# Scaling the attention probabilities on GpSimd instead of VectorE

## The reference

```python
# for each of 4 blocks of 128 queries, 16 heads of 64
logits = einsum("bqhd,bkhd->bhqk", q_blk, kf) * scale
logits = logits + (cq_blk[..., :, None] - ck[:, :, None, :])
logits = where(kpos <= qpos, logits, NEG_INF)
p = softmax(logits, axis=-1)
o = einsum("bhqk,bkhd->bqhd", p, vf)
```

## Time and profile before

| | |
|---|---|
| median of 3 runs | 2271.0 us (2269.18 to 2271.35) |
| the profiled execution, its time | 2272.01 us |
| its span | 2270.2 us |
| granted TensorE clock, mean | 0.996 |
| TensorE busy | 2247.9 us (99%) |
| VectorE busy | 1278.5 us (56%) |
| ScalarE busy | 819.6 us (36%) |
| GpSimd busy | 1.4 us (0%) |

### The profile page before, as it was taken

The page is one execution under the profiler, slowest core; times in us unless marked ns, Lnnn a source line. Parts: engine busy times, 40 slices in busy tenths (PEclk is TensorE's granted clock), DMA queues, the critical chain, the costliest instruction groups (busy, mean ns, idle before and its releaser), DMA issues.

```text
span 2270.2 us, 27725 instructions
## 1 busy us (share of the span) xinstructions
PE 2247.9 (99%) x10130; PEld 1845.0 (81%) x10130; DVE 1278.5 (56%) x1820; ACT 819.6 (36%) x1125; POOL 1.4 (0%) x6
## 2 busy tenths in 40 slices
PE   9999999999999999999999999999999999999998
PEld 7788878778888888888888888888888888888887
DVE  8878784758555345646454455555335555553544
ACT  6676473635333212224222223233212233221222
POOL 0000000000000000000000000000000000000000
PEclk9999999999999999999999999999999999999999
DMA  5233212122223222232322223222222232222322
GB/s 179 95 102 107 90 46 85 64 79 93 75 74 101 94 102 93 92 102 84 111 94 93 102 91 104 75 75 88 98 94 101 91 102 96 94 92 102 102 93 74
DMA packets 59507, 211.62 MB, mean 93 GB/s; under 512 B 6736, under 2 KB 7120, under 8 KB 59280
## 3 DMA queue, kind: packets, MB, share of 16 engines
q1 hardware_dynamic: 59040, 208.83, 27.2%
q0 software_dynamic: 224, 1.31, 0.2%
q10 hardware_dynamic: 144, 0.12, 0.0%
HBM read 208.14 MB, written 2.10 MB: 93 GB/s over the span
## 4 chain that ended last, share of the span: by engine, by line
PE 85%; DVE 2%; ACT 1%; issue 0%; DVEq 0%; ACTq 0%
PE bank L634 25%; PE bank L636 25%; PE bank L635 25%; PE bank L629 2%; PE bank L630 2%; PE bank L631 2%; PE bank L848 2%; ACT arena L1150 1%; PE bank L808 1%; PE bank L837 1%; PE bank L794 1%; PE bank L859 0%; DVE arena L1635 0%; DVE y_lo L1604 0%; PE bank L776 0%
## 5 line engine op out<-in xcount | busy, mean ns | idle before, releaser
L1298 DVE TENSOR_TENSOR w_lo<-w_raw,w_hi 128x1024 fp32r<-128x1024 f32 x387 | 467.6, 1223 | 775.3 <-ACT w_hi L934 774.4
L934 ACT ACTIVATE w_hi<-w_raw 128x1024 fp32r<-128x1024 f32 x387 | 403.9, 1057 | 944.8 <-PE bank L636 915.9
L634 PE MATMUL bank<-h_hi,w_hi 128*128 128x512 f32 x1788 | 701.2, 392 | 5.0 <-DVE arena L1333 2.0
L635 PE MATMUL bank<-h_lo,w_hi 128*128 128x512 f32 x1788 | 696.4, 389 | 0.0
L636 PE MATMUL bank<-h_hi,w_lo 128*128 128x512 f32 x1788 | 696.2, 389 | 0.0
L634 PE MATMUL bank<-y_hi,w_hi 128*128 128x512 f32 x1056 | 411.0, 389 | 1.6 <-DVE w_lo L1298 1.3
L636 PE MATMUL bank<-y_hi,w_lo 128*128 128x512 f32 x1056 | 410.8, 389 | 0.0
L635 PE MATMUL bank<-y_lo,w_hi 128*128 128x512 f32 x1056 | 410.8, 389 | 0.0
L634 PEld LDWEIGHTS bank<-h_hi,w_hi 128*128 128x128 f32 x1788 | 336.1, 188 | 77.8 <-DVE w_lo L1298 4.9
L635 PEld LDWEIGHTS bank<-h_lo,w_hi 128*128 128x128 f32 x1788 | 336.1, 188 | 70.9 <-issue 1.7
L636 PEld LDWEIGHTS bank<-h_hi,w_lo 128*128 128x128 f32 x1788 | 336.0, 188 | 70.3
(11 more groups left out here) (216 smaller groups left out, 1401.0 us busy)
## 6 DMA issues: line engine op xcount, KB each, us to landing
w_raw<-in_stream SPq DMA_DIRECT2D x389, 512.0 KB, 3.3
x<-in_x_t SPq DMA_DIRECT2D x8, 256.0 KB, 7.3
out_t<-x SPq DMA_DIRECT2D x8, 256.0 KB, 2.2
arena<-in_consts POOLq DMA_DIRECT2D x1, 1024.0 KB, 5.2
w_raw<-in_stream SPq DMA_DIRECT2D x2, 256.0 KB, 4.8
arena<-in_positions POOLq DMA_DIRECT2D x1, 256.0 KB, 6.2
vec_t<-in_vecs ACTq DMA_DIRECT2D x1, 112.5 KB, 3.1
ident<-in_consts SPq DMA_DIRECT2D x1, 64.0 KB, 6.9
```

Of the source, the lines that this page charges most:

```text
L634: pe.matmul(out, w_hi[:, slot, w], a_h, start=first, stop=False)
L635: pe.matmul(out, w_hi[:, slot, w], a_l, start=False, stop=False)
L934: A.activation(w_hi[:, slot, :], w_raw[:, slot, :], ACT.Copy).then_inc(hi_ready, 1)
L1298: V.tensor_tensor(w_lo[:, slot, :], w_raw[:, slot, :], w_hi[:, slot, :].bitcast(F32), ALU.subtract).then_inc(lo_ready, 1)
```

## The change

The four multiplications of each head move from VectorE's `normalise` into a new function `scale_probs` of GpSimd, which is called once at the start of each half of the attention. The reciprocal stays on VectorE and raises a new semaphore, `sums_inverted`, by one for each head; GpSimd waits for it and does the four multiplications, each of which raises `probs_ready` by one. `turn` now waits for four of these for each head instead of five.

```diff
+        sums_inverted = sem("sums_inverted")
...
         def _(pool):
             T = Tally()
+
+            def scale_probs():
+                for hh in range(HEADS // 2):
+                    sm = 32 * (hh % 2)
+                    pool.wait_ge(sums_inverted, T.value("halves", hh + 1, HEADS // 2))
+                    for t in range(TT):
+                        at = P * t * (t + 1) // 2
+                        p_t = probs[:, hh % 2, at:at + P * (t + 1)]
+                        nc.gpsimd.tensor_scalar(p_t, p_t, small[:, sm + 12 + t:sm + 13 + t], None, ALU.mult)\
+                            .then_inc(probs_ready, 1)
+
             for item in steps:
+                if isinstance(item, Bind) and item.name == "half" and not T.loops and T.fixed["halves"] < 2:
+                    scale_probs()
...
                 def turn(hh):
-                    pe.wait_ge(probs_ready, heads(5, 5 * hh + 5))
+                    pe.wait_ge(probs_ready, heads(4, 4 * hh + 4))
...
                 def normalise(hh):
                     sm = 32 * (hh % 2)
                     dve.wait_ge(exp_ready, heads(4, 4 * hh + 4))
-                    V.reciprocal(small[:, sm + 12:sm + 16], small[:, sm + 8:sm + 12]).then_inc(probs_ready, 1)
-                    dve.wait_ge(probs_ready, heads(5, 5 * hh + 1))
-                    for t in range(TT):
-                        at = P * t * (t + 1) // 2
-                        p_t = probs[:, hh % 2, at:at + P * (t + 1)]
-                        V.tensor_scalar(p_t, p_t, small[:, sm + 12 + t:sm + 13 + t], None, ALU.mult)\
-                            .then_inc(probs_ready, 1)
+                    V.reciprocal(small[:, sm + 12:sm + 16], small[:, sm + 8:sm + 12]).then_inc(sums_inverted, 1)
```

## The result

The changed kernel takes 2306.91 us (2306.41 to 2307.36, 4 runs) against 2270.31 (2269.18 to 2271.35, 4 runs) for the one before: a ratio of 1.0159, 95% interval 1.0147 to 1.0172, 36.6 us slower. The forecast was 2281 in 2270 to 2312; direction and range held, the size did not, a loss of 10 forecast and 37 measured.

What follows compares the result with a forecast made beforehand. The prediction took TensorE, 99% busy, to bound the kernel. Per half, 4 x 1.53 - 3 x 0.58 = 4.4, twice 8.8 us; with 1.65 for one clock fall, 2271.0 + 10.4 gave 2281, range 2270 to 2312.

Steps and rivals of the forecast that it cites:

- A to B: Leg from an even head's transposes' start to the next odd head's: 3.43 us before, predicted 4.96, 1.53 longer.
- D: Time of one head's four scalings on GpSimd, 1280 columns in all; estimated 2.7 us, against 1.27 on VectorE.
- the even leg: From an odd head's transposes' start to the next even head's: 6.19 us before, predicted 5.61, hiding the even head's scaling.
- rival 2: Scaling so slow (D over 3.35) that it sets both legs: 2308 at D = 5, 2358 at 8.6; chance 0.2.
- signs of being wrong: D outside 2.2 to 3.3, the clock falling at each pair, or the values product still ending the wait before odd heads.
- 1.6 ns a column, D = 2.05 + 0.62 = 2.7: GpSimd's scaling of a head, put between VectorE's two-input subtract (1.04 ns a column) and its scan (2.06).
- The clock: TensorE's granted clock falling toward 1.2 GHz after idling before odd heads; one fall over six such places booked, 1.65 us.
- rival 3: The clock falls before every odd head: six more falls at 1.65, 9.9 us on top of 8.8, 2290; chance 0.12.
- Head 0: First head of each half: scaling hidden behind the v product's tail and copies, cost 0; 1.0 us at risk from subtracts.
- The 0.58 us: Predicted shortening of each leg from odd to even head, 6.19 to 5.61, as VectorE's maxima start earlier.
- Rival 4: VectorE and GpSimd hold each other up, maxima run after the scaling as now: 3.5 us more, 2285; chance 0.05.

## Why the prediction was right in direction and wrong in size

**The chain held.** "A to B becomes D + 2.26": with the measured 4.27 that is 6.53, and the trace has 6.48. That D under 3.35 hides behind the even leg, and that above it both legs are D + 2.26, was rival 2, and it is what happened (6.41 to 6.47). The formula with D = 4.27 gives 8 x 3.1 + 6 x 0.34 = 26.8; the legs without the clock show 5.3 + 18.3 + 1.7 = 25.3. The kernel with its clock held is 26.7 slower than before by the medians and 24.6 by the spans, but that it comes so near is in part luck: it has head 0's loss in it, and it is spared the fall behind head 7, 1.5 and 1.2 us in the two halves, that the kernel before pays. That 2307 lies in the range is no merit of the sum either: the high end, 2312, stood for a D of 5 with two or three falls, and it was 4.27 with five. Of the prediction's own signs of being wrong two came true, D outside 2.2 to 3.3 and falls at nearly every pair.

**The step that failed is the price D**, the term "1.6 ns a column, D = 2.05 + 0.62 = 2.7". It measured 2.5 ns a column and 0.29 a piece, 4.27 in a row: above the scan's 2.06, well below the reciprocal's 6.2. I put an engine that had shown no row between two rows of a different engine, and took the middle of them as if it were likely; what the trace supported was only the wide bound. This term alone made 25.3 out of 8.8, 16.5 us of the miss; the clock, 6.5, and head 0, 1.6, are the rest of the 24.7 by the spans. The rule in the Trainium skill, "GPSIMD Engine Reference", section "Engine selection", that one-input work is at roughly line rate on GpSimd, is not borne out: by it, with the page's clock of 1.2 GHz, 1280 columns would take 1.07 us (an estimate), and 3.7 times that was measured even with a constant scalar. Its other half, that elementwise work belongs on VectorE, held: the ratio here was 4.27 to 1.27.

**The clock**, booked as one fall, 1.65, was 8.1 over the kernel before (6.7 in the legs, 1.4 behind head 7). The price of a fall was about right, 0.7 to 2.0 a leg; their number was not, five of six legs. The idle stretch was 3.1 us and not 1.6, and behind the stretches of 1.07 to 1.77 us that the kernel with odd heads' reciprocals ahead had, no fall came. So the number followed from D: rival 3 came true on top of rival 2. As rivals I had priced them as alternatives, which they are not; only the high end of the range put the two together.

**Head 0**, booked at 0 with 1.0 at risk, was 1.6 in the first half by the start of its transposes and nothing in the second. The mechanism was named, and its cover was too short for a D of 4.27 plus 1.56.

**The 0.58 us** of a freed VectorE were never seen in the changed kernel, since the scaling set that leg. Where the odd heads alone were on GpSimd and the clock stayed up, the leg was 5.61, the very sum. Rival 4 did not occur in the pairs: the four maxima beside GpSimd's scaling took 1.69 us, before 1.68, and the copy, which stood beside it with the odd heads' reciprocals ahead, 0.56 as before.

## What to carry to other kernels

An engine that stands idle is not a cheap place for work on a chain: here 1.27 us of relief a head bought 3 us of wait before each odd one, and the same instructions where most of their time was hidden (even heads) cost 7.5 us in all against 33.6. Before moving work, look at what stands in front of it in its queue: putting the scaling ahead of one waiting copy gained more (4 us) than any share given to GpSimd, most of it by a wait short enough that the clock stayed up behind it. And when a wait on TensorE grows, price its length and the clock together, as one case: here the longer wait brought both.

## What was not expected of the hardware

- GpSimd's one-input float32 multiply runs at 2.5 ns a column plus 0.29 us a piece (0.21 with a constant), against VectorE's 0.5 ns a column.
- Two legs behind the same idle stretch of 3.1 us cost 7.56 and 8.42 us: the lower clock was granted within 324 to 329 us the first time and from 338 to 346 the second.
- A VectorE scaling and a GpSimd scaling that start together lengthen each other by part of an instruction (880 for 605 ns, 528 for 415), while a GpSimd piece beside two VectorE subtracts with two SBUF inputs took 1.56 us more, and with a constant as its scalar 0.51.
